# Layer 0's closing product in three passes, block-wise stores, and a first modulation summed in the two halves of the array

## The chip, the core and the metric

The kernel runs on one core of a Trainium2 chip. The metric is the device time of one launch in microseconds (us); the runs shown are the median of three. Engine names in the rows: PE is TensorE's matmuls and PEld its weight loads, DVE is VectorE, ACT is ScalarE, POOL is GpSimd, SP is the queue on which most transfers are issued.

## What is computed

Two blocks of a small transformer stand behind each other, in float32, with 256 latent tokens, 256 context tokens and a model width of 1024. Only three places of it matter here.

```
mod_l = split(silu(c) @ ada_w[l] + ada_b[l], 6)          # and mod_c from c_ctx
hl = modulate(x_lat, norm_g[l, 0], mod_l[0], mod_l[1])    # rms_norm(x) * (1 + scale) + shift
...
mix_c, mix_l = even_mixer(hc, hl, ...)                    # 4 mLSTM heads and 8 window-attention heads
x_lat = x_lat + mod_l[2] * (mix_l @ w_out[l])             # the closing product of the mixer
x_lat = x_lat + mod_l[5] * conv_ffn(modulate(x_lat, norm_g[l, 1], mod_l[3], mod_l[4]), ...)
```

Parts 0 and 1 of the first `mod` (shift and scale of layer 0, for latent and context) are needed before any product on `h` can start. In layer 0 the closing product `mix @ w_out[0]` is made for latent and context tokens, 512 columns; in layer 1 for the 256 latent ones. The second block ends in a layer norm and a gated sum, which gives the output.

## The kernel before

Everything lies feature-major: `x`, `h` and `mix` hold 8 blocks (index `k`, `KD` = 8) of 128 features by 512 tokens. A weight tile is 128 by 1024 (512 KB), that is 8 stationary blocks of 128 by 128 for one output block. Each engine has its own program, written out in order by hand; they meet in semaphores (`mark` raises one, `at` names the value to wait for).

**The weight ring.** All weight tiles come through `RING`, 7 places of 512 KB, in the order of the list `TILES`. `sync_program` issues tile t on SP when tile t-7 has been released; what releases it is named with the tile (its product, or the pass over it that takes its rest).

**Two ways to multiply.** `pe_product` (L246) multiplies in plain float32: each matmul is recorded as two LDWEIGHTS and two MATMUL. `pe_product3` (L264 to L266) makes three passes instead, on operands that are split beforehand in a rounded part (type fp32r) and the rest: rounded weights by rounded data, rounded weights by the rest of the data, rest of the weights by rounded data. Each of the three is one record. The split of a weight tile is an ACT copy (`act_round`, L273), then a subtraction on DVE (`dve_rest`, L279) or POOL (`pool_rest`, L285), into one of three pairs `HI`, `LO`.

**The start.** `pe_start` sums the first modulation: 16 tiles of `ada_first`, numbered from 0, per tile 8 matmuls with a stationary of 2 columns (the two conditions, `cs`) and 128 columns of the tile moving, into 2 rows of a bank (L393). Ahead of tile 12 stands the mean of the squares of x (L436). ACT copies the rows out after tiles 3, 7, 11 and 15 (L365); ahead of the last copy stand a table load and the two steps of the reciprocal root (L442, L444), by which DVE and POOL normalise x (L468, L464). At last PE turns the rows into columns with 16 small transposes (L398), DVE adds the bias (L417), forms the gains (L428) and scales `h` (L477), and the first product on `h` starts (L246).

**The end of the mixer.** The last head ends with the numerators (PE L853), the denominators (ACT L895) and divisions on DVE, the turned probabilities (PE L721, copies L747 and L749, scaled by DVE L676), the attention sums of 64 rows each (PE L731, two heads in turns in the two halves of the columns), `mixed_attention` (L976) and `mixed_heads` (L979). Then `pe_wout(0)` makes 8 output blocks of 8 plain matmuls each, block 0 at L1008 with its waits inside, blocks 1 to 7 by `pe_product`. After each block DVE adds it to x (L1054, `residual`), ACT squares (L1025), DVE sums the squares (L1038). In between DVE works through two pairs of modulation tiles, `dve_ada` (L335, L338). After the last block come a mean, a reciprocal root, and the modulated h, split in two, for the up product of the feed-forward (L1131 to L1133 for its first three tiles in one loop, then `pe_product3`).

**The end.** `pool_close` writes the last sum block by block (`closed`), and SP stores the whole output in one transfer when all 8 are closed.

## Time and profile before

| | before |
|---|---|
| median of the three runs, us (lowest, highest) | 1690.59 (1689.98, 1692.39) |
| the profiled execution's own time, us | 1693.57 |
| its span in the trace, us | 1692.3 |
| PE busy | 1593.9 us (94%) |
| DVE busy | 1098.3 us (65%) |
| ACT busy | 712.1 us (42%) |
| POOL busy | 463.6 us (27%) |

Where PE is busy for 94% of the span, the time gets shorter where PE's work gets less, or where PE waits and the wait goes. Busy shares don't tell which; the chain of waits and the timeline at the three places do. The times in the rows below count from the start of the span.

### The profile page before, as it was taken

Reading aid. Unit: us, or ns where it says so; the run is one execution under the profiler, and the core shown is the slowest. Engines: PE = TensorE matmul, PEld = TensorE weight load, DVE = VectorE, ACT = ScalarE, POOL = GpSimd, SP = SyncE. Lnnn points to the kernel's source line nnn. Section 1 sums busy time; section 2 is a strip of 40 time slices with the busy share of each in tenths; the row PEclk is TensorE's granted clock in tenths of the full one; section 3 lists DMA queues with packets and bytes.
Section 4 is the critical chain, followed back from the end, with each engine's and each line's share of the span. In section 5 each row is a group of like instructions: output and inputs, shape, how many; then the busy total and the mean of one; then the engine's idle time right before and its main releaser. Section 6 shows DMA issues by size and latency. Waiting matters only on the chain.

```text
span 1692.3 us, 24887 instructions
## 1 busy us (share of the span) xinstructions
PE 1593.9 (94%) x9516; PEld 1300.4 (77%) x9516; DVE 1098.3 (65%) x2015; ACT 712.1 (42%) x1333; POOL 463.6 (27%) x375
## 2 busy tenths in 40 slices
PE   7999999989999999988999999999999999999888
PEld 5555566448888888866667899998888888898777
DVE  4567887558877788747777788655454545453763
ACT  1432433143333332344442555544444444454544
POOL 1012102002222210115530111025555555522651
PEclk9899999999999999999999999999999999999999
DMA  9323213224333356502234455544333334344230
GB/s 346 138 99 113 99 64 137 100 74 147 138 137 140 148 203 209 196 33 100 88 113 162 172 186 178 187 176 132 133 135 129 134 127 135 120 136 148 94 131 26
DMA packets 63831, 231.23 MB, mean 137 GB/s; under 512 B 7408, under 2 KB 8432, under 8 KB 63456
## 3 DMA queue, kind: packets, MB, share of 16 engines
q1 hardware_dynamic: 60800, 218.65, 36.8%
q0 software_dynamic: 2192, 6.29, 1.1%
q10 hardware_dynamic: 720, 4.68, 0.7%
q8 instruction: 76, 1.25, 0.3%
q14 instruction: 43, 0.35, 0.1%
HBM read 228.55 MB, written 1.05 MB: 136 GB/s over the span
## 4 chain that ended last, share of the span: by engine, by line
PE 82%; DVE 8%; ACT 5%; issue 3%; POOL 1%; DMA 0%; ACTq 0%; DVEq 0%; POOLq 0%
PE ps L264 12%; PE ps L246 12%; PE ps L266 12%; PE ps L265 12%; PE ps L1241 4%; PE ps L1240 4%; PE ps L1239 4%; PE ps L254 2%; PE ps L731 2%; PE ps L393 2%; PE ps L721 2%; DVE big L676 2%; ACT big L657 2%; PE ps L624 1%; PE ps L308 1%
## 5 line engine op out<-in xcount | busy, mean ns | idle before, releaser
L279 DVE TENSOR_TENSOR weights_rest<-ring,weights_rounded 128x1024 fp32r<-128x1024 f32 x193 | 267.6, 1389 | 66.5 <-ACT weights_rounded L273 66.4
L273 ACT ACTIVATE weights_rounded<-ring 128x1024 fp32r<-128x1024 f32 x231 | 241.9, 1053 | 120.6 <-PE ps L1241 94.1
L266 PE MATMUL ps<-h_hi,weights_rest 128*128 128x512 f32 (+1 forms) x640 | 215.1, 336 | 0.0
L265 PE MATMUL ps<-h_lo,weights_rounded 128*128 128x512 f32 (+1 forms) x640 | 215.1, 336 | 0.0
L264 PE MATMUL ps<-h_hi,weights_rounded 128*128 128x512 f32 (+1 forms) x640 | 215.1, 336 | 0.0
L1225 POOL TENSOR_TENSOR big<-scratch 128x512 f32<-128x512 f32 (+1 forms) x44 | 64.2, 1460 | 406.4 <-DVE scratch L1211 406.4
L1165 ACT ACTIVATE scratch<-ps,vectors 128x512 f32<-128x512 f32 (+1 forms) x88 | 59.2, 672 | 191.4 <-PE ps L266 182.5
L285 POOL TENSOR_TENSOR weights_rest<-ring,weights_rounded 128x1024 fp32r<-128x1024 f32 x38 | 91.2, 2402 | 168.6 <-ACT weights_rounded L273 168.6
L246 PE MATMUL ps<-h,ring 128*128 128x512 f32 x288 | 131.4, 612 | 2.2 <-DVE h L477 2.2
L265 PEld LDWEIGHTS ps<-h_lo,weights_rounded 128*128 128x128 f32 x640 | 121.5, 190 | 12.6
L266 PEld LDWEIGHTS ps<-h_hi,weights_rest 128*128 128x128 f32 x640 | 121.5, 190 | 12.5
L264 PEld LDWEIGHTS ps<-h_hi,weights_rounded 128*128 128x128 f32 x640 | 121.5, 190 | 12.4
L338 DVE SCALAR_TENSOR_TENSOR ring<-ring,cond_rows 128x1024 f32<-128x1024 f32 x80 | 123.1, 1539 | 2.8
L1239 PE MATMUL ps<-hid_rounded,weights_rounded 128*128 128x512 f32 (+1 forms) x352 | 120.7, 343 | 3.8 <-DVE hid_rest L1300 3.8
L1241 PE MATMUL ps<-hid_rounded,weights_rest 128*128 128x512 f32 (+1 forms) x352 | 119.1, 338 | 0.0
L1240 PE MATMUL ps<-hid_rest,weights_rounded 128*128 128x512 f32 (+1 forms) x352 | 119.0, 338 | 0.0
L246 PEld LDWEIGHTS ps<-h,ring 128*128 128x128 f32 x288 | 55.9, 197 | 72.3 <-issue 69.6
L335 DVE SCALAR_TENSOR_TENSOR junk<-ring,cond_rows 128x1024 f32<-128x1024 f32 x80 | 102.3, 1278 | 1.0 <-POOL scratch L1066 1.0
L1208 DVE SCALAR_TENSOR_TENSOR scratch<-ps,vectors,scratch 128x510 f32<-128x510 f32 (+1 forms) x88 | 53.8, 611 | 63.7 <-ACT scratch L1165 63.6
L264 PE MATMUL ps<-x_hi,weights_rounded 128*128 128x256 f32 x280 | 83.4, 298 | 1.1 <-ACT scratch L1739 1.1
L264 PE MATMUL ps<-x_hi,a_rounded 128*128 128x256 f32 x248 | 74.6, 301 | 5.2 <-ACT scratch L1746 5.2
L266 PE MATMUL ps<-x_hi,weights_rest 128*128 128x256 f32 x280 | 79.1, 282 | 0.0
(366 smaller groups left out, 3916.3 us busy)
## 6 DMA issues: line engine op xcount, KB each, us to landing
ring<-in_up SPq DMA_DIRECT2D x88, 512.0 KB, 3.9
ring<-in_ada_rest SPq DMA_DIRECT2D x80, 512.0 KB, 4.5
ring<-in_a_in SPq DMA_DIRECT2D x80, 512.0 KB, 3.5
ring<-in_down SPq DMA_DIRECT2D x44, 512.0 KB, 3.7
ring<-in_even SPq DMA_DIRECT2D x20, 512.0 KB, 3.8
ring<-in_ada_first SPq DMA_DIRECT2D x16, 512.0 KB, 8.1
ring<-in_wout SPq DMA_DIRECT2D x16, 512.0 KB, 3.5
ring<-in_odd SPq DMA_DIRECT2D x16, 512.0 KB, 3.5
```

Of the source, the lines that this page charges most:

```text
L246: ins = te.matmul(bank[:, 0:n], w[:, k, :], rhs(k), start=k == 0, stop=k == KD - 1)
L264: te.matmul(bank[:, 0:n], wh[:, k, :], hi(k), start=k == 0, stop=False)
L265: te.matmul(bank[:, 0:n], wh[:, k, :], lo(k), start=False, stop=False)
L266: ins = te.matmul(bank[:, 0:n], wl[:, k, :], hi(k), start=False, stop=k == KD - 1)
L273: sc.activation(pair[0], place(*key), ACT.Copy).then_inc(*mark("rounded", *key))
L279: ve.tensor_tensor(pair[1], place(*key), pair[0].bitcast(F32), ALU.subtract).then_inc(*mark("rest", *key))
L285: po.tensor_tensor(pair[1], place(*key), pair[0].bitcast(F32), ALU.subtract).then_inc(*mark("rest_pool", *key))
L335: ve.scalar_tensor_tensor(JUNK, w, 1.0, CREP[:, 0:D], ALU.mult, ALU.mult, accum_out=SUMS[:, 2 * j:2 * j + 1]).then_inc(*mark("mod_products ...
L338: ve.scalar_tensor_tensor(w, w, 1.0, CREP[:, D:2 * D], ALU.mult, ALU.mult, accum_out=SUMS[:, 2 * j + 1:2 * j + 2]).then_inc(*mark("mod_sum ...
L1239: te.matmul(b, wh[:, e, :], hi, start=j == 0, stop=False)
L1240: te.matmul(b, wh[:, e, :], lo, start=False, stop=False)
L1241: ins = te.matmul(b, wl[:, e, :], hi, start=False, stop=j == FB - 1)
```

## The change

1. **Start.** `cs` becomes 64 columns for each `k` (2 with the conditions, 62 of zeros, cleared by POOL). The matmuls of even `k` write rows 0 to 63 of the bank and those of odd `k` rows 64 to 127, each half with its own columns of the array, and the halves are added later: the 16 turning steps become matmuls with 128 rows as stationary and a matrix `V_SUM` of two columns (ones in rows 0 and 64, and in rows 1 and 65) moving. They wait for the four copies one by one.
2. **Closing product of layer 0.** It is made in three passes. `mix` is split into `MIX_HI` (in the place of `h`, which is free by then) and `MIX_LO` (in place): ACT rounds the 8 blocks, POOL takes the rests of 0, 1, 2, 4, 5, 6 and DVE those of 7 and 3. The weight tiles are split too: rounded on ACT, the rests of tiles 0 to 2 on POOL, of 3 to 7 on DVE, three pairs in turn. Blocks 0 and 1 are made in one loop over `k`.
3. **Pairs for the up product.** Its first four tiles get pairs of their own in `BIG`, in both layers, since `HI` and `LO` are in use until the closing product ends.
4. **Stores.** SP stores each of the 8 output blocks when it is closed, and waits for the last.

```diff
@@ wout_tiles
-            tile(("wout", layer, b), f"wout{layer}", b, "product", "wout", layer, b)
+            tile(("wout", layer, b), f"wout{layer}", b, wout_rest(b) if layer == 0 else "product", "wout", layer, b)
@@ sync_program
             sp.wait_ge(*at("closed", 1, k))
-        sp.dma_start(out, xv[:, :, LAT]).then_inc(*mark("stored", step=16))
-        sp.wait_ge(*at("stored"))
+            sp.dma_start(out[:, k, :], xk(k)).then_inc(*mark("stored", k, step=16))
+        sp.wait_ge(*at("stored", KD - 1))
@@ pe_start
             for k in range(KD):
-                ins = te.matmul(BANK[b][0:2, 128 * (s % 4):128 * (s % 4) + 128], cs[:, 2 * k:2 * k + 2], w[:, k, :],
-                                start=k == 0, stop=k == KD - 1)
+                half = slice(64 * (k % 2), 64 * (k % 2) + 64)
+                ins = te.matmul(BANK[b][half, 128 * (s % 4):128 * (s % 4) + 128], cs[:, k, :], w[:, k, :],
+                                start=k < 2, stop=k >= KD - 2)
             ins.then_inc(*mark("product", "ada_first", s))
-        te.wait_ge(*at("rows_copied", 3))
-        for j in range(16):
-            ins = te.transpose(BANK[2][:, 2 * j:2 * j + 2], rows2[0:2, 128 * j:128 * j + 128], ident[0:2, 0:2])
+        for g in range(4):
+            te.wait_ge(*at("rows_copied", g))
+            for j in range(4 * g, 4 * g + 4):
+                ins = te.matmul(BANK[2][:, 2 * j:2 * j + 2], rows2[:, 128 * j:128 * j + 128], v(V_SUM, 2), start=True,
+                                stop=True)
@@ act_even
+        if i == AH - 1:
+            for b in range(2):
+                act_round(("wout", 0, b), pair(b), wout_free(b))
         act_exps(us)
...
+            if i == AH - 1 and t == 3:
+                for k in range(3):
+                    act_mix(k, at("mixed_heads", k))
             sc.wait_ge(*at("numerators", i, t))
...
         head_norm()
+        if i == AH - 1:
+            act_mix(4, at("mixed_attention", 0))
         weigh_copies(sc, 1, E, groups0(i), TB0, PT0, only=(5,))
+        if i == AH - 1:
+            for k in (5, 6, 7):
+                act_mix(k, at("mixed_attention", k - 4))
+            act_round(("wout", 0, 2), pair(2), wout_free(2))
+            act_mix(3, at("mixed_heads", 3))
@@ pool_even
+        if i == AH - 1:
+            for b in range(2):
+                pool_rest(("wout", 0, b), pair(b), wout_free(b))
+            for k in (0, 1, 2, 4, 5, 6):
+                mix_rest(po, k)
@@ new
+    def pe_wout_split():
+        for b in range(2):
+            te.wait_ge(*at(wout_rest(b), "wout", 0, b))
+        for x, k in enumerate((0, 1, 2, 4, 5, 6, 7, 3)):
+            te.wait_ge(*at("rest_pool" if mix_on_pool(k) else "h_rest", "mix", k))
+            hi, lo = mix_parts(k)
+            for b in range(2):
+                wh, wl = (v3(w, 128)[:, k, :] for w in pair(b))
+                te.matmul(BANK[b], wh, hi, start=x == 0, stop=False)
+                te.matmul(BANK[b], wh, lo, start=False, stop=False)
+                ins = te.matmul(BANK[b], wl, hi, start=False, stop=x == KD - 1)
+                if x == KD - 1:
+                    ins.then_inc(*mark("product", "wout", 0, b))
+        for b in range(2, KD):
+            if b >= 4:
+                te.wait_ge(*at("residual", 0, b - 4))
+            pe_product3(("wout", 0, b), pair(b % PAIRS), BANK[b % 4], TOK, lambda k: mix_parts(k)[0],
+                        lambda k: mix_parts(k)[1], wout_rest(b))
@@ act_wout
+            if layer == 0 and b + 3 < KD:
+                act_round(("wout", layer, b + 3), pair(b % PAIRS), wout_free(b + 3))
@@ dve_wout
+        if layer == 0:
+            mix_rest(ve, 7)
+            mix_rest(ve, 3)
         ve.wait_ge(*at("wout_cleared", layer))
...
+            if layer == 0 and b + 3 < KD:
+                dve_rest(("wout", layer, b + 3), pair(b % PAIRS), wout_free(b + 3))
@@ pool_wout
         po.memset(acc_o[:, 0:n], 0.0).then_inc(*mark("wout_cleared", layer))
+        if layer == 0:
+            pool_rest(("wout", 0, 2), pair(2), wout_free(2))
```

How the order moves on the engines for which PE waits. ACT at the end of the last head, before: the copies of the denominators (L895), the turned copies (L747), the heads' squares and norm (L903 to L915).

```order
L895 ACTIVATE scratch<-ps 128x2 x4
L747 ACTIVATE scratch<-ps 128x512
L903 ACTIVATE scratch<-scratch 128x128 x4
L747 ACTIVATE scratch<-ps 128x512
L909 ACTIVATE scratch<-scratch,eps 128x4
L911 ACTIVATE scratch<-scratch 128x4
L915 ACTIVATE scratch<-scratch 128x128 x4
L747 ACTIVATE scratch<-ps 128x512
```

The same place on ACT after the change (L895 is now L912, L747 is L758; L1037 rounds a block of `mix`):

```order
L912 ACTIVATE scratch<-ps 128x2 x3
L1037 ACTIVATE mix_hi<-mix 128x512 x3
L912 ACTIVATE scratch<-ps 128x2
L758 ACTIVATE scratch<-ps 128x512
L920 ACTIVATE scratch<-scratch 128x128 x4
L758 ACTIVATE scratch<-ps 128x512
L926 ACTIVATE scratch<-scratch,eps 128x4
L928 ACTIVATE scratch<-scratch 128x4
L932 ACTIVATE scratch<-scratch 128x128 x4
L1037 ACTIVATE mix_hi<-mix 128x512
L758 ACTIVATE scratch<-ps 128x512
L1037 ACTIVATE mix_hi<-mix 128x512 x3
```

Three roundings now stand ahead of the last of the four denominator copies, and one ahead of the last turned copy. DVE in the closing product, before (L335 and L338 are modulation tiles, L1054 the residual, L1038 the sum of squares), from the residuals of blocks 0 and 1 to that of block 2:

```order
L1054 SCALAR_TENSOR_TENSOR x<-ps,mod,x 128x256 x4
L1038 TENSOR_TENSOR scratch<-scratch 128x512
L335 SCALAR_TENSOR_TENSOR junk,mod_sums<-ring,cond_rows 128x1024
L338 SCALAR_TENSOR_TENSOR ring,mod_sums<-ring,cond_rows 128x1024
L335 SCALAR_TENSOR_TENSOR junk,mod_sums<-ring,cond_rows 128x1024
L338 SCALAR_TENSOR_TENSOR ring,mod_sums<-ring,cond_rows 128x1024
L1054 SCALAR_TENSOR_TENSOR x<-ps,mod,x 128x256 x2
L1038 TENSOR_TENSOR scratch<-scratch 128x512
```

The same place on DVE after (L1123 is the residual, L1104 the sum of squares, L282 the rest of a weight tile, L338 and L341 modulation tiles):

```order
L1123 SCALAR_TENSOR_TENSOR x<-ps,mod,x 128x256 x2
L282 TENSOR_TENSOR weights_rest<-ring,weights_rounded 128x1024
L1123 SCALAR_TENSOR_TENSOR x<-ps,mod,x 128x256 x2
L1104 TENSOR_TENSOR scratch<-scratch 128x512
L282 TENSOR_TENSOR weights_rest<-ring,weights_rounded 128x1024
L338 SCALAR_TENSOR_TENSOR junk,mod_sums<-ring,cond_rows 128x1024
L341 SCALAR_TENSOR_TENSOR ring,mod_sums<-ring,cond_rows 128x1024
L338 SCALAR_TENSOR_TENSOR junk,mod_sums<-ring,cond_rows 128x1024
L341 SCALAR_TENSOR_TENSOR ring,mod_sums<-ring,cond_rows 128x1024
L1123 SCALAR_TENSOR_TENSOR x<-ps,mod,x 128x256 x2
L1104 TENSOR_TENSOR scratch<-scratch 128x512
L282 TENSOR_TENSOR weights_rest<-ring,weights_rounded 128x1024
```

The rest of tile b+3 stands behind the residual of block b, and that of tile 5 behind two modulation tiles as well.

## Rows read from the trace of the kernel before

**Rows 1.** The page, part 4: the chain that ended last, by engine

```profile
PE 82%; DVE 8%; ACT 5%; issue 3%; POOL 1%; DMA 0%; ACTq 0%; DVEq 0%; POOLq 0%
```

**Rows 2.** Chain of waits in the first 110 us: start us, us, what

```profile
7.10 23.74 PE ps L393 x192
...
31.89 7.09 PE ps L393 x64
...
40.83 0.20 DVE mod L417
...
42.98 15.51 PE ps L246 x32
```

**Rows 3.** Timeline, 0 to 20 us: PE's weight load waits for a tile

```profile
14.95 5.11 PEld L393 LDWEIGHTS ps<-ring,scratch 128*2 128x2 f32 x48 [0.28 <-DMA ring<-in_ada_first]
```

**Rows 4.** Windows: PE, PEld, DVE, ACT, POOL busy (count), clock, DMA share, GB/s

```profile
14.00:20.00 6.00, 6.00 (x56) 4.46 (x55) 5.73 (x9) 0.59 (x1) 0.00 (x0) 1.00 1.03 412
...
43.00:46.00 3.00, 3.00 (x4) 1.45 (x5) 2.05 (x6) 2.43 (x5) 0.29 (x1) 0.50 0.98 368
```

**Rows 5.** Timeline, 20 to 40 us: the copy after tile 11, the normalising of x

```profile
30.87 0.59 ACT L365 ACTIVATE scratch<-ps 2x512 f32<-2x512 f32 x1 [6.40 <-PE ps L393]
...
34.15 5.83 DVE L468 TENSOR_TENSOR h<-x,rsqrt 128x512 f32<-128x512 f32 x6 [8.76 <-ACT rsqrt L444]
34.20 3.43 POOL L464 TENSOR_TENSOR h<-x,rsqrt 128x512 f32<-128x512 f32 x2 [33.33 <-ACT rsqrt L444]
```

**Rows 6.** Timeline from 38.5 us: the last three of L468

```profile
38.10 1.88 DVE L468 TENSOR_TENSOR h<-x,rsqrt 128x512 f32<-128x512 f32 x3
```

**Rows 7.** Timeline, 1166 to 1176 us, PE: sums in the halves of the columns

```profile
1170.43 1.31 PE L731 MATMUL ps<-big,scratch 128*64 128x256 f32 x16
```

**Rows 8.** Window on L398 alone: PE, PEld busy (count), clock, DMA share, GB/s

```profile
39.64:40.62 0.98, 0.97 (x16) 0.97 (x16) 1.00 0.84 313
```

**Rows 9.** Chain of waits, 285 to 400 us

```profile
304.26 6.87 PE ps L1008 x16
311.13 48.08 PE ps L246 x112
...
367.41 0.43 PE ps L1132
...
384.97 0.23 PE ps L264
...
390.41 0.23 PE ps L264
```

**Rows 10.** Timeline of ACT, 290 to 305 us: the last denominator copy

```profile
295.28 0.17 ACT L895 ACTIVATE scratch<-ps 128x2 f32<-128x2 f32 x1 [1.39 <-PE ps L853]
```

**Rows 11.** Timeline of DVE, 295 to 304 us: the last probabilities

```profile
298.75 1.12 DVE L676 TENSOR_SCALAR big<-big,stats 128x256 f32<-128x256 f32 x4
```

**Rows 12.** Groups of DVE by line and shape, 304 to 362 us: busy, mean ns

```profile
L1054 DVE SCALAR_TENSOR_TENSOR x<-ps,mod,x 128x256 f32<-128x256 f32 x16 | 7.0, 480 | 30.3 <-PE ps L246 30.0 <-PE ps L1008 0.3
L338 DVE SCALAR_TENSOR_TENSOR ring<-ring,cond_rows 128x1024 f32<-128x1024 f32 x4 | 4.9, 1224 | 0.1
...
L1038 DVE TENSOR_TENSOR scratch<-scratch 128x512 f32<-128x512 f32 x7 | 4.8, 681 | 0.0
L279 DVE TENSOR_TENSOR weights_rest<-ring,weights_rounded 128x1024 fp32r<-128x1024 f32 x3 | 3.5, 1217 | 0.0
```

**Rows 13.** Groups of ACT by line and shape, 304 to 362 us

```profile
L1025 ACT ACTIVATE scratch<-x 128x512 f32<-128x512 f32 x8 | 5.0, 630 | 51.6 <-DVE x L1054 51.6
L273 ACT ACTIVATE weights_rounded<-ring 128x1024 fp32r<-128x1024 f32 x3 | 2.9, 1041 | 0.0
```

**Rows 14.** The page, part 5: a weight tile's rest on POOL

```profile
L285 POOL TENSOR_TENSOR weights_rest<-ring,weights_rounded 128x1024 fp32r<-128x1024 f32 x38 | 91.2, 2402 | 168.6 <-ACT weights_rounded L273 168.6
```

**Rows 15.** DMA issues of the whole run: size, median us from issue to landing

```profile
big<-in_rpb POOLq DMA_DIRECT2D x32, 64.0 KB, 2.2
...
out<-x SPq DMA_DIRECT2D x1, 1024.0 KB, 5.4
...
scratch<-in_masks POOLq DMA_DIRECT2D x1, 256.0 KB, 3.1
```

More of the change, by code:

```diff
@@ L144, in build, with wout_rest @@
     ODD_ADA = [(68, 69), (70, 71), (72,), (73,)]
+    def wout_rest(b):
+        return "rest_pool" if b < 3 else "rest"
     def wout_tiles(layer):
@@ L359, in act_start @@
         sc.wait_ge(*at("vectors_in"))
-        sc.activation(cs, v(V_C, 16), ACT.Silu).then_inc(*mark("cond_act"))
+        sc.wait_ge(*at("cond_cleared"))
+        sc.activation(cs[:, :, 0:2], v3(v(V_C, 16), 2), ACT.Silu).then_inc(*mark("cond_act"))
         for g in range(4):
@@ L991, in pool_even, with wout_free, mix_parts @@
         pool_rope(("even", i), at("normed", "even", i, 0), q0[:, CTX:TOK], ROPE1, t2)
+        if i == AH - 1:
[3 more added lines that the diff above has]
+                mix_rest(po, k)
     FIRST = 3
     acc_o, sq_o = SCR[:, 0:TOK], [SCR[:, TOK:2 * TOK], SCR[:, 2 * TOK:3 * TOK]]
+    def wout_free(b):
+        return [at("product", "wout", 0, b - PAIRS)] if b >= PAIRS else []
+    def mix_parts(k):
+        return MIX_HI[:, k * TOK:(k + 1) * TOK], MIX_LO[:, k * TOK:(k + 1) * TOK]
@@ new lines, in act_mix, with mix_on_pool, mix_rest @@
+    def act_mix(k, event):
+        sc.wait_ge(*event)
+        sc.activation(mix_parts(k)[0], MIX[:, k * TOK:(k + 1) * TOK], ACT.Copy).then_inc(*mark("h_rounded", "mix", k))
+    def mix_on_pool(k):
+        return k % 4 < 3
+    def mix_rest(eng, k):
+        hi, lo = mix_parts(k)
+        eng.wait_ge(*at("h_rounded", "mix", k))
+        ins = eng.tensor_tensor(lo, MIX[:, k * TOK:(k + 1) * TOK], hi.bitcast(F32), ALU.subtract)
+        ins.then_inc(*mark("rest_pool" if mix_on_pool(k) else "h_rest", "mix", k))
@@ L998, in pe_wout @@
     def pe_wout(layer):
         n = TOK if layer == 0 else SEQ
-        order, waits = ((0, 1, 2, 4, 5, 6, 7, 3), {0: at("mixed_heads", AH - 2), 7: at("mixed_attention", AH - 1), 3: at(
-            "mixed_heads", AH - 1)}) if layer == 0 else ((0, 1, 2, 3, 4, 5, 6, 7), {0: at("mixed_global", 3),
-                                                         4: at("mixed_near", 2), 7: at("mixed_near", 3)})
-        w = v3(place("wout", layer, 0), 128)
-        te.wait_ge(*loaded("wout", layer, 0))
-        for x, k in enumerate(order):
-            if k in waits:
-                te.wait_ge(*waits[k])
-            ins = te.matmul(BANK[0][:, 0:n], w[:, k, :], mixk(n)(k), start=x == 0, stop=x == KD - 1)
@@ L1009, in pe_wout @@
-        ins.then_inc(*mark("product", "wout", layer, 0))
-        for b in range(1, KD):
-            if b >= 4:
-                te.wait_ge(*at("residual", layer, b - 4))
-            pe_product(("wout", layer, b), BANK[b % 4], n, mixk(n))
+        if layer == 0:
+            pe_wout_split()
+        else:
+            waits = {0: at("mixed_global", 3), 4: at("mixed_near", 2), 7: at("mixed_near", 3)}
+            for b in range(KD):
+                if b >= 4:
+                    te.wait_ge(*at("residual", layer, b - 4))
+                pe_product(("wout", layer, b), BANK[b % 4], n, mixk(n),
+                           lambda k, b=b: [waits[k]] if b == 0 and k in waits else [])
@@ L1089, in halves @@
                 yield k, s, c, slice(k * n + c, k * n + c + 256)
-    UP_THIRD = (rounded("up_rounded_3", "big", 9216, D), rounded("up_rest_3", "big", 10240, D))
+    MIX_HI, MIX_LO = rounded("mix_hi", "h", 0, KD * TOK), rounded("mix_lo", "mix", 0, KD * TOK)
+    UP_FIRST = [(rounded(f"up_rounded_{j}", "big", c, D), rounded(f"up_rest_{j}", "big", c + D, D))
+                for j, c in enumerate((5120, 7168, 9216, 1024))]
     def up_pair(j):
-        return UP_THIRD if j == FIRST else pair((j if j < FIRST else j - 1) % PAIRS)
+        return UP_FIRST[j] if j <= FIRST else pair((j - 1) % PAIRS)
     def up_free(layer, j):
-        if j == FIRST:
-            return [at("mixed_near", 3)] if layer else [at("mixed_heads", AH - 1)]
+        if j > FIRST + PAIRS:
+            return [at("product", "up", layer, j - PAIRS)]
         if j > FIRST:
-            return [at("product", "up", layer, j - (PAIRS if j > FIRST + PAIRS else PAIRS + 1))]
-        return [at("product", "down", 0, FB - 1)] if layer else []
+            return [at("product", "wout", layer, KD - 1)]
+        return [at("mixed_near", 3)] if layer else [at("mixed_heads", AH - 1)]
     def down_pair(j):
```

11 lines of the change are left out of this document (8 added, 3 removed).

## The prediction

> **What bounds the kernel now.** First I read the chain of waits by engine [rows 1]: PE carries 82% of it, so a change counts where it takes work from PE or ends a wait of PE. Then the same chain in order of time, at the three places.
>
> *Start.* PE sums 12 tiles in 23.74 us and the last 4 in 7.09, that is 1.77 each [rows 2]. The timeline shows PE waiting for a tile at 14.95 [rows 3]: from there to 30.84 there are nine tiles of 1.77, so this is tile 3. The transfers meanwhile run at 412 GB/s with their engines full [rows 4]: 0.524 MB lands each 1.27 us. PE is the slower of the two, and transfers are right behind it. After tile 11 come ACT's copy (30.87), the root, and DVE's normalising from 34.15 for 5.83 us [rows 5], to 39.98. The bias waits for the turned rows until 40.83, and PE starts its first product at 42.98 [rows 2], at the lower clock (0.50 of full in 43 to 46 us, [rows 4]).
>
> *Closing product.* 16 records of L1008 and 112 of L246 take 54.95 us [rows 9], 6.87 a block, without a wait. DVE and ACT wait for PE there (30.3 and 51.6 us of idle time, [rows 12, 13]).
>
> *End.* One store of 1 MB lands 5.4 us after its issue [rows 15], and nothing lies beside it.
>
> **Start, term by term.** Two sums in the two halves of the columns: L731 is the same form (64 columns each, in turns). Its 16 records [rows 7], twelve with 128 columns moving and four with 256, would take 12 x 0.11 + 4 x 0.22 = 2.2 us one after the other (0.11 is 7.09 / 64, [rows 2]); they take 1.31, less some 0.16 for the last one's tail: 1.9 times as fast. A tile then costs PE 0.93 us, below the 1.27 at which it lands. So PE follows the transfers: tile 11 lands at 14.95 + 8 x 1.27 = 25.1 and is summed at 26.2 instead of 30.84. The chain behind it is unchanged: 3.3 us from copy to normalising, 5.83 of normalising [rows 5], end at 35.4. The other branch: tile 15 lands at 30.2, is summed at 31.3; the turning is now 32 records (two per plain matmul) where there were 16 at 0.061 each [rows 8], 2.0 us; at 0.11 each it would be 3.5. The last eight wait for a copy of 0.6. It ends by 33.3, at the dear price by 34.8, before 35.4 both times: the doubled turning costs nothing, because DVE's normalising hides it; without that cover it would cost up to 2. The bias starts at 35.4 instead of 40.83: **5.4 us**. What is late next is the clock. PE now stands nearly idle from 33.3 to 37.6 (before: 40.8 to 43.0), and in the 15.51 us of the first 32 records [rows 2] at 0.43 each (6.87 / 16, [rows 9]) there are already 1.75 us of lower clock. It can last as long again or vanish: -1.75 to +1.75, I take **-0.5**. The wider copies (128 rows for 2) move the same 512 columns and cost nothing; POOL's clearing lies before the vectors land.
>
> **Closing product.** Three passes: from the first record of up tile 3 to that of tile 4 it is 390.41 - 384.97 = 5.44 us for 24 matmuls [rows 9], a block of the same size. Eight blocks: 43.6 against 54.95, a gain of 11.4. Against it stand the waits:
> - *Before the product.* ACT was free from 293.89 to 295.28 [rows 10]. Three roundings of 0.6 (a 512-column copy, [rows 13]) now end at 295.7 and delay the last denominators, on which DVE's chain to the last copy hangs: 0.5. The roundings and rests of weight tiles 0 and 1 fall where ACT waits for an output and for DVE, and are hidden: without that cover 2.1.
> - *POOL beside DVE.* While POOL normalised its two blocks, three of DVE's took (5.83 - 1.88) / 3 = 1.32 us each; with POOL idle, 1.88 / 3 = 0.63 [rows 5, 6]. POOL now takes three rests of about 1.2 (half of 2402 ns, [rows 14]) from 294.5 to 298.2 or later, and L676 stands at 298.75 with 1.12 us [rows 11]. If it falls beside POOL wholly it doubles: 0 to 1.2, I take 0.7. The Trainium skill ("SBUF — State Buffer", section "SBUF: two separate sides") says that DVE and GpSimd take a shared port pair in turns, as an exclusive lock for a whole instruction. By that rule each of the four L676 could wait out a whole POOL rest, and the sum would be worse by up to 4 us; the rows show a doubling, and POOL should be through by then.
> - *Inside.* With P the end of blocks 0 and 1 (10.9 us after the start): residual 0.9, square 0.63, rounding 1.04, rest 1.22 [rows 12, 13] make tile 3 ready at P + 3.9, needed at P + 5.4. Residual 1, square, rounding and rest 4: P + 7.75, needed at P + 10.9. Then four modulation passes of 1.22 and residual 2, its square, the rounding of 5 and its rest: P + 16.5, needed at P + 16.35. That is the tightest place: 0.2. Tiles 6 and 7 are ready at about P + 20.5 and P + 24.5, needed at P + 21.8 and P + 27.2. `mix` 7 and 3 are needed 8.2 us after the start, DVE has them at about 5.
> - *After it.* The rests for the up product reach into the last residual: 0.3.
>
> Sum: 11.4 - 0.5 - 0.7 - 0.2 - 0.3 = **9.7 us**. The ring is no bound: tile 3 is issued when the first modulation tile of this stage is summed, some 6 us before its rounding. Ends: nothing lost, 11.4; or start late by 3 and DVE's work late for three blocks by 1 each: 5. The separate pairs move no wait of PE, since the up product's first tiles were rounded at the same place before: 0.
>
> **Stores.** The last one is 128 KB. The nearest rows are 64 KB with 2.2 and 256 KB with 3.1 [rows 15]; I take 2.6 for 5.4: **2.8 us**, ends 2.3 and 3.2. The other seven lie beside the closing blocks. The Trainium skill ("DMA: Bandwidth & Descriptors") gives a fixed cost of about 2.0 us and 436 GB/s; that makes 2.3, an estimate, and the sum 0.3 better.
>
> **Sum.** 5.4 - 0.5 + 9.7 + 2.8 = 17.4. The profiled execution (1693.57, its span and 1.3 around it) becomes 1676.2; it lies 3.0 above the median of the runs, 1690.59, which becomes **1673.2**.
>
> **Rivals.**
> - *A, the first sums gain little.* If PE waits for tiles at the lower clock, a tile costs it 1.86, tile 11 is summed at 29.4 and the turned rows come last: gain 0 to 2 there, time 1677 to 1678.5. For it: PE now has gaps between tiles. Against: when it slows, it falls behind the transfers and has no gaps left.
> - *B, the preparation doesn't keep up.* If DVE's passes beside POOL take 1.5 times as long, tiles 5, 6 and 7 are late by 1 to 2 us each, and the product's start by 3: gain 5, time 1677 to 1681. For it: a margin below zero at tile 5. Against: DVE is idle for 30 us of this stage.
> - *C, more than the sum.* Clock and POOL cost nothing or give back: 1669 to 1670.5.
> - *D, slower.* The lower clock stays through the closing product. At the lower level a pass takes 0.43, not 0.227 [rows 9]: 192 x 0.2 = 39 us more, net 22 slower, 1712. It decides once the lower level covers 85 of the 192 passes (17.4 / 0.2). Against it: PE goes into the product from work at full clock, and never waits long in it.
> - *E, no change:* only if start and product both fail.
>
> **How the numbers follow.** Forecast (1670.5 to 1677) 0.60, A 0.12, B 0.18, C 0.06, D 0.03, E 0.01. The predicted time is the forecast's. 1669 to 1680 leaves out D, E and the far end of B, with a tail on either side, about 0.1 to 0.15. A measurement tells 0.2% (3.4 us) from no change: faster 0.95, same 0.02, slower 0.03.
>
> **What would show it.** Right: L365's third copy near 26.3, L417 near 35.5; the records of the first sums in pairs, with waits for `ring` between tiles; PE's closing product near 44 us with at most a short wait before block 5; the last landing about 2.6 us after its issue. Wrong: L417 released by PE's turned rows (A), waits of PE for `weights_rest` before blocks 5 to 7 or a long stretch of DVE behind POOL near 299 us (B), a clock of 0.5 inside the product (D).

## The result, and the profile after

The changed kernel takes 1672.34 us in the median of four runs (1670.31 to 1673.68), the kernel before 1690.64 beside it. The ratio is 0.9894, with a 95% interval from 0.988 to 0.9908: 18.3 us faster, predicted were 17.4. The same kernel once more, `a0_after` below, gave 0.9896 [0.9881, 0.991].

The profiled execution is the slowest of the four (1673.68, span 1672.3). By its page PE still carries the chain that ended last, with 81% against 82% [rows 1]. The three places follow, each read against its rows of before.

**Start.** The chain of waits, first 57 us (start, us, what), against [rows 2]:

```profile
2.12 12.70 DMA ring<-in_ada_first
14.86 4.18 PE ps L402 x48
19.06 8.57 DMA ring<-in_ada_first
...
28.80 3.81 PE ps L402 x64
32.61 5.03 PE ps L408 x32
37.66 0.20 DVE mod L428
...
39.81 16.50 PE ps L249 x32
```

The transfers now stand where PE's sums stood: two stretches of DMA, 21.3 us together. The timeline of PE shows the sums (L402) waiting for tiles. The last column is the idle time before a group and what ended it:

```profile
14.86 6.21 PE L402 MATMUL ps<-ring,scratch 128*64 128x128 f32 x80 [0.81 <-DMA ring<-in_ada_first]
21.26 1.09 PE L402 MATMUL ps<-ring,scratch 128*64 128x128 f32 x16 [0.18 <-DMA ring<-in_ada_first]
23.83 1.09 PE L402 MATMUL ps<-ring,scratch 128*64 128x128 f32 x16 [1.48 <-DMA ring<-in_ada_first]
...
26.40 1.09 PE L402 MATMUL ps<-ring,scratch 128*64 128x128 f32 x16 [0.19 <-DMA ring<-in_ada_first]
```

Tiles 3 to 8 come at the pace of the transfers: (21.26 - 14.86) / 5 = 1.28 us. Tile 9 comes 2.57 after tile 8, one slot late, and tiles 10 and 11 keep that distance. So the sum of tile 11 begins at 26.40, and its copy stands at 27.54 where the prediction had 26.3. The copy and what hangs on it, answering to [rows 5] (first row ACT, the others DVE):

```profile
27.54 0.60 ACT L372 ACTIVATE scratch<-ps 128x512 f32<-128x512 f32 x1 [5.82 <-PE ps L402]
```

```profile
30.83 5.85 DVE L479 TENSOR_TENSOR h<-x,rsqrt 128x512 f32<-128x512 f32 x6 [5.54 <-ACT rsqrt L455]
37.66 0.19 DVE L428 TENSOR_TENSOR mod<-ps,vectors 128x32 f32<-128x32 f32 x1 [0.98 <-PE ps L408]
```

In this execution the bias (L428) stood 0.98 us idle behind the turned rows, at 37.66 instead of 40.83 [rows 2]. That is 3.2 us sooner; predicted were 5.4.

**Clock.** Windows of the same kernel (PE, PEld, DVE, ACT, POOL busy with counts, granted clock, DMA share, GB/s), against the second line of [rows 4]:

```profile
34.60:39.80 5.20, 3.02 (x16) 2.96 (x16) 4.08 (x10) 1.57 (x4) 1.56 (x3) 0.51 1.03 417
39.80:44.90 5.10, 5.09 (x6) 2.17 (x7) 2.08 (x6) 2.46 (x6) 0.32 (x1) 0.50 0.86 353
```

From 34.6 to 44.9 us PE ran at 1.2 GHz, three times as long as before at this place, so the first 32 records took 16.50 us instead of 15.51. They end at 56.31, against 42.98 + 15.51 = 58.49 before: 2.2 us are left of the start in this execution.

**Closing product.** PE's groups by line from 299.5 to 343.1 us (busy, mean ns, idle before), where [rows 9] had 54.95 us:

```profile
L267 PE MATMUL ps<-mix_hi,weights_rounded 128*128 128x512 f32 x48 | 18.7, 389 | 0.0
```

The groups of the other two passes, L268 and L269, have the same figures. The loop over the first two blocks (L1056 to L1058) has 48 records with 6.2 to 6.3 us for each of its lines. There is no idle time ahead of any pass. The chain has the product's start and the last residual:

```profile
299.52 0.24 PE ps L1056
...
343.52 0.47 DVE x L1123
```

From start to last residual it takes 343.52 - 299.52 = 44.0 us. Before it was 359.64 - 304.26 = 55.38; the start is in [rows 9], and the last residual in the same chain is

```profile
359.64 0.48 DVE x L1054
```

**End.** The DMA issues of the last 30 us, and the chain's last row, against [rows 15]:

```profile
out<-x SPq DMA_DIRECT2D x8, 128.0 KB, 1.9
```

```profile
1669.66 0.72 POOL x L2118
```

The span ends at 1672.3, 1.9 us behind the last block. The last block of before, in its chain:

```profile
1686.06 0.72 POOL x L2043
```

There it was 1692.3 - (1686.06 + 0.72) = 5.5. That gives 3.6; predicted were 2.8.

### The profile page after: what moved, and what is told of

It is laid out like the page before. It is cut to its first block, busy times and chain, and to the rows that moved or that the text cites. A ratio compares the mean times of both kernels' runs of the same rounds, so it can differ in the third digit from the quotient of the medians.

```text
span 1672.3 us, 25099 instructions
## 1 busy us (share of the span) xinstructions
PE 1572.5 (94%) x9596; PEld 1310.1 (78%) x9596; DVE 1109.3 (66%) x2022; ACT 724.2 (43%) x1349; POOL 476.7 (29%) x385
## 3 DMA queue, kind: packets, MB, share of 16 engines
HBM read 228.55 MB, written 1.05 MB: 137 GB/s over the span
## 4 chain that ended last, share of the span: by engine, by line
PE 81%; DVE 8%; ACT 5%; issue 3%; DMA 1%; POOL 1%; SPq 0%; ACTq 0%; DVEq 0%; POOLq 0%
PE ps L267 13%; PE ps L269 12%; PE ps L268 12%; PE ps L249 9%; PE ps L1314 4%; PE ps L1315 4%; PE ps L1316 4%; PE ps L257 2%; DVE big L687 2%; PE ps L742 2%; PE ps L732 2%; ACT big L668 2%; PE ps L311 1%; PE ps L635 1%; DMA ring<-in_ada_first 1%
## 5 line engine op out<-in xcount | busy, mean ns | idle before, releaser
L282 DVE TENSOR_TENSOR weights_rest<-ring,weights_rounded 128x1024 fp32r<-128x1024 f32 x192 | 267.9, 1397 | 72.7 <-ACT weights_rounded L276 72.7
L268 PE MATMUL ps<-h_lo,weights_rounded 128*128 128x512 f32 (+1 forms) x640 | 215.0, 336 | 0.0
L269 PE MATMUL ps<-h_hi,weights_rest 128*128 128x512 f32 (+1 forms) x640 | 215.0, 336 | 0.0
L288 POOL TENSOR_TENSOR weights_rest<-ring,weights_rounded 128x1024 fp32r<-128x1024 f32 x41 | 98.4, 2402 | 177.2 <-ACT weights_rounded L276 177.2
L268 PEld LDWEIGHTS ps<-h_lo,weights_rounded 128*128 128x128 f32 x640 | 121.5, 190 | 12.6
L269 PEld LDWEIGHTS ps<-h_hi,weights_rest 128*128 128x128 f32 x640 | 121.5, 190 | 12.5
L341 DVE SCALAR_TENSOR_TENSOR ring<-ring,cond_rows 128x1024 f32<-128x1024 f32 x80 | 123.1, 1539 | 2.8
L338 DVE SCALAR_TENSOR_TENSOR junk<-ring,cond_rows 128x1024 f32<-128x1024 f32 x80 | 102.1, 1276 | 0.4 <-POOL scratch L1137 0.4
L268 PE MATMUL ps<-x_lo,weights_rounded 128*128 128x256 f32 x280 | 79.7, 285 | 0.0
L269 PE MATMUL ps<-x_hi,weights_rest 128*128 128x256 f32 x280 | 79.7, 284 | 0.0
```

Source lines behind the costliest of these rows:

```text
L268: te.matmul(bank[:, 0:n], wh[:, k, :], lo(k), start=False, stop=False)
L269: ins = te.matmul(bank[:, 0:n], wl[:, k, :], hi(k), start=False, stop=k == KD - 1)
L282: ve.tensor_tensor(pair[1], place(*key), pair[0].bitcast(F32), ALU.subtract).then_inc(*mark("rest", *key))
L288: po.tensor_tensor(pair[1], place(*key), pair[0].bitcast(F32), ALU.subtract).then_inc(*mark("rest_pool", *key))
L338: ve.scalar_tensor_tensor(JUNK, w, 1.0, CREP[:, 0:D], ALU.mult, ALU.mult, accum_out=SUMS[:, 2 * j:2 * j + 1]).then_inc(*mark("mod_products ...
L341: ve.scalar_tensor_tensor(w, w, 1.0, CREP[:, D:2 * D], ALU.mult, ALU.mult, accum_out=SUMS[:, 2 * j + 1:2 * j + 2]).then_inc(*mark("mod_sum ...
```

## The experiments

### The three parts one by one

Each part alone on top of the kernel before, all three on one chip.

`e1_stores` stores by block and changes nothing else:

```diff
-        sp.dma_start(out, xv[:, :, LAT]).then_inc(*mark("stored", step=16))
-        sp.wait_ge(*at("stored"))
+            sp.dma_start(out[:, k, :], xk(k)).then_inc(*mark("stored", k, step=16))
+        sp.wait_ge(*at("stored", KD - 1))
```

> The kernel before with the block-wise stores alone. In the profile after the change the last store of 128 KB landed 1.9 us after its issue, and before the change the one store took 5.4. Theory (the end is an independent term): 3.5 us faster, last landing 1.9 us after issue, everything ahead unchanged. Rival (seven earlier stores cost something beside the closing blocks, or the issue of the last one queues behind them): less than 2.5 us faster, and closing blocks more than 3.74 us apart.

Measured: 1685.86 against 1690.03, ratio 0.9975 [0.9964, 0.9985], 4.2 us faster (2.5 to 6.1 by the interval), where 3.5 were expected. The trace has it at the place: the last block is closed at 1681.82 + 0.72, the span ends at 1684.5, 2.0 behind it instead of 5.5. The last closing blocks start 3.74 us apart, so the earlier stores hold nothing up and the rival is out.

`e2_wout` has the product in three passes and the separate pairs, with the old start and the old store:

```diff
-            tile(("wout", layer, b), f"wout{layer}", b, "product", "wout", layer, b)
+            tile(("wout", layer, b), f"wout{layer}", b, wout_rest(b) if layer == 0 else "product", "wout", layer, b)
...
+    def pe_wout_split():
```

> The kernel before with the closing product in three passes and the separate pairs, and with the start and the store as before. Theory (passes times 0.227 us, ACT's roundings delay the start of the product by 0.5 to 0.9): the product from its first record to the last residual takes 44.0 us instead of 55.4, the product starts 0.5 to 0.9 later than in the kernel before apart from differences of the clock, and the whole is 10.5 us faster (9.5 to 11.5), a stretch of lower clock more or less adding or taking 1.7. Rival (part of the 11.4 us belongs to the earlier start): below 9 us.

Measured: 1676.38, ratio 0.992 [0.9906, 0.9933], 13.6 us faster (11.3 to 15.9 by the interval), above the 9.5 to 11.5 that were expected; the rival, below 9, is out. This execution and that of `e1_stores` reach the last head within 0.01 us of each other (L853 at 288.06, here L858 at 288.05), which makes them a clean pair. The chain of `e1_stores`:

```profile
288.06 4.48 PE ps L853 x40
...
301.56 6.87 PE ps L1008 x16
...
356.94 0.48 DVE x L1054
```

The chain of `e2_wout`:

```profile
288.05 2.92 PE ps L858 x26
...
301.91 0.23 PE ps L1050
...
345.90 0.47 DVE x L1117
```

The product begins 301.91 - 301.56 = 0.35 us later and takes 43.99 instead of 55.38.

Little of the 0.35 is ACT's. Its three roundings end just as the last denominators are ready: DVE starts on them at 292.81 instead of 292.77, 0.04 later. The rest comes from two DVE instructions that stand beside POOL's rests of `mix`. The first (L977) takes 0.24 us instead of 0.16. The second is the first L675, 0.38 instead of 0.15, and it ends when POOL does:

```profile
295.14 0.38 DVE L675 TENSOR_TENSOR stats<-stats 128x1 f32<-128x1 f32 x1
```

```profile
291.75 3.75 POOL L1039 TENSOR_TENSOR mix_lo<-mix,mix_hi 128x512 fp32r<-128x512 f32 x3 [7.21 <-ACT mix_hi L1031]
```

Net gain at the last residual: 11.04 us, where the prediction's term was 9.7. The measured 13.6 lies above it, with 11.04 just outside its interval. The two traces differ by 12.45 when the last block is closed (1682.54 against 1670.09); the 1.4 in between come after this place. `e1_stores` has 3.4 us more of the lower clock in that part (34.1 against 30.7), which can be worth up to 1.7; no run isolates it.

`e3_start` has the new start alone:

```diff
-                ins = te.matmul(BANK[b][0:2, 128 * (s % 4):128 * (s % 4) + 128], cs[:, 2 * k:2 * k + 2], w[:, k, :],
-                                start=k == 0, stop=k == KD - 1)
+                half = slice(64 * (k % 2), 64 * (k % 2) + 64)
+                ins = te.matmul(BANK[b][half, 128 * (s % 4):128 * (s % 4) + 128], cs[:, k, :], w[:, k, :],
+                                start=k < 2, stop=k >= KD - 2)
```

> The kernel before with the start alone. Theory (transfers and the turning bound it: tile 11 is summed near 27.5, the turned rows come last): the bias starts near 37.7 instead of 40.83, and the first product's 32 records end about 2.2 us earlier (56.3). Time 2 to 3 us faster, plus or minus 3.4 by how long the lower clock lasts further on. Rival (the shorter low stretches near 75 and 90 us in the profile after the change were caused by the earlier start): 5 us faster and more, with low stretches near 75 and 90 us of 3.4 us each in this profile as well.

Measured: 1686.43, ratio 0.9979 [0.997, 0.9988], 3.6 us faster (2.0 to 5.1 by the interval), where 2 to 3 were expected, with the bias near 37.7. The bias in its timeline of DVE:

```profile
36.73 0.18 DVE L423 TENSOR_TENSOR mod<-ps,vectors 128x32 f32<-128x32 f32 x1
```

Here the bias has no bracket: it follows the normalising (30.95, for 5.85 us) at once, 0.9 us sooner than in the first profile of the changed kernel. The first product's 32 records end at 38.59 + 16.28 = 54.87, in `e1_stores` at 43.07 + 15.67 = 58.74: 3.9 us sooner. So the first profile of the changed kernel, with 2.2, showed less than this part is usually worth.

The three gains add up to 4.2 + 13.6 + 3.6 = 21.4 us, 3 more than all three bring together. Most of the surplus goes with the clock. Over the runs of this study the time of one and the same kernel falls by some 1.06 us for each 0.001 of mean granted clock, and the runs of `e1_stores` (0.9869 in the mean) and `e2_wout` (0.9865) had more of it than those of the kernel before beside them (0.9856), those of `e3_start` less (0.9844). Brought to one clock by this figure, the gains are 2.6, 12.2 and 4.9, together 19.7, and that of `a0_after` is 18.9. These are estimates from the times and clocks of all runs; single runs lie 0.5 us around them. Within that the parts add up: `e2_wout` lies 1.1 above its trace instead of 2.6, and `e1_stores` 0.9 below its own.

### The changed kernel once more, and three ways to mend its start

`a0_after` is the changed kernel again, on the chip of the next three kernels.

> The changed kernel once more, on the chip and in the call of the next three, so that they can be compared with it. Theory: 18 us below the kernel before. The bias of the first modulation starts at 36.6 us, when DVE's normalising ends, if TensorE's clock falls behind the turning, and at 37.7 if it falls inside it, as in the first profile of this kernel (0.213 us a record instead of 0.112).

Measured: 1671.01 (1670.38 to 1672.63) against 1688.59. The clock fell at 35.8, when the turning was nearly through, and the bias stood behind the normalising. Its chain at the start and at the last residual:

```profile
36.72 0.11 DVE mod L428
...
38.74 15.96 PE ps L249 x32
...
341.88 0.47 DVE x L1123
```

Its 32 records end at 54.70. In four of the six profiled executions with this start (`e3_start`, `a0_after`, `e7_mix_late`, `e8_pad_tile5`) the normalising sets the bias; in the first profile and in `e10_fill_only` the turned rows come last, by 0.98 and 0.26 us. So this one is of the more frequent kind, and the sum below is read from it.

`e4_turn_early` turns groups 0 to 2 of the rows among the sums:

```diff
+            if s in (6, 10, 15):
+                turn({6: 0, 10: 1, 15: 2}[s])
...
+        turn(3).then_inc(*mark("rows_turned"))
```

> The turning of groups 0 to 2 of the rows stands ahead of tiles 6, 10 and 15, so that only 8 of 32 records are left behind the last copy. Theory (turned rows came last in the first profile, DVE's normalising 1 us before them): the bias starts at 36.6 to 36.7 wherever the clock falls, 1.0 us sooner than in the first profile of the changed kernel and not sooner than where the clock fell later; the whole 0 to 1 us shorter. Rival (turning is not what sets the bias): nothing. Rival 2 (24 records of 0.11, that is 2.7 us, now delay tiles 6, 10 and 15 past their landing): copy 2 and so the normalising come up to 1 us later, since a tile takes PE 0.9 of the 1.27 us at which it lands.

Measured: 1671.38 (1668.42 to 1673.46), ratio 0.9893 [0.9875, 0.9912], no difference that can be told. The bias stands at 36.78. What the early turning would save where the clock falls inside it, as in the first profile, this execution does not show. Tile 11's copy came at 27.65 against 27.57, so the early turning was hidden behind the waits for tiles, and rival 2 is out.

`e5_root_early` also computes the mean and the root ahead of the copy behind tile 11:

```diff
-            if g == 3:
+            if g == 2:
...
+            if s == 11:
+                te.wait_ge(*at("consts_in", "first"))
+                pe_mean((0, 0), ACC, TOK, at("square_sum", "x", KD - 1))
```

> As the one before, and the mean is computed ahead of tile 11, while its load is awaited, with ACT's root ahead of the copy behind that tile. Theory: with the turning out of the way DVE's normalising sets the bias; it hangs on mean, root (1.28 + 0.70 + 0.64 us) and the copy of 0.6 ahead of them, so it starts 1.3 to 2 us sooner, and the bias at 34.6 to 35.4: the whole 1.3 to 3 us below the changed kernel. Rival (something else, as the first weights of the product or the last tiles' sums, comes last): below 0.5 us. The last tile is summed at 32.6, its copy ends at 33.3, 8 records follow: 34.3, so that this bound lies just below.

Measured: the bias stands at 35.35, 1.4 us sooner, as expected. The whole took 1670.61 (1669.22 to 1672.94), ratio 0.9893 [0.9878, 0.9908]: not the 1.3 to 3 us less that were expected, but no difference that can be told. The chain says where it went:

```profile
35.35 0.20 DVE mod L432
...
37.51 16.80 PE ps L249 x32
```

and the windows of the same execution:

```profile
19.30:36.40 17.10, 15.25 (x206) 13.19 (x202) 12.40 (x19) 4.76 (x7) 3.90 (x3) 1.00 1.03 408
36.40:43.20 6.80, 5.69 (x7) 2.52 (x8) 3.18 (x8) 3.56 (x8) 1.42 (x3) 0.50 1.03 423
```

The product begins 1.2 us sooner (37.51 against 38.74 in `a0_after`), but more of it lies in the stretch at the lower clock, and its 32 records take 16.80 us instead of 15.96. They end at 54.31, only 0.4 sooner.

`e6_fill` adds three matmuls, whose result is not read, in PE's gap:

```diff
+        for _ in range(3):
+            te.matmul(BANK[3], mean_d, xv[:, 0, :], start=True, stop=True)
```

> As the one before, with three fp32 matmuls of 512 columns more behind the turning, into a bank that is not read, which fill some 2.7 us of PE's idle time before the first product. Theory (the lower clock in the first product follows PE's idle time from 33 to 38 us): less of the 10.2 us of lower clock that the first profile of the changed kernel shows, the first 32 records of the product in 14 to 15.5 us instead of 16.5, whole 1 to 2.5 us less than without. Rival (PE is still partly idle from 15 to 33 us, and that suffices): the same 16.3 to 16.7 us, the lower clock only begins at another time; difference to the one before below 0.5.

Measured: 1667.62 (1665.58 to 1669.20), ratio 0.9873 [0.9859, 0.9888]. All four runs lie below all four of `a0_after` and of `e5_root_early`; against the latter the median is 3.0 us lower, more than the 1 to 2.5 expected. Chain and windows of the profiled execution:

```profile
35.17 2.68 PE ps L416 x6
37.85 13.73 PE ps L249 x32
```

```profile
36.00:43.00 7.00, 7.00 (x18) 3.17 (x17) 3.44 (x8) 3.81 (x8) 1.68 (x3) 1.00 1.02 420
```

Until 35.2 us this kernel does what the one before it does. Then PE works instead of standing, the clock stays at 2.4 GHz through the product's start, and 32 records take 13.73. The first product ends at 51.58, 3.1 us sooner than in `a0_after`, though it starts only 0.9 sooner. It has the lowest median of the study. The profiled execution is the fastest of its four, at a mean granted clock of 0.990; the others have 0.986 to 0.988, so this good case is not the rule.

### How sure the filler is

`e9_fill_one` is the same with one filling matmul (`range(1)`).

> The kernel with early turning and root, and one filling matmul (0.9 us) instead of three (2.7 us). Theory (the fall of the clock at 36.4 us follows the idle stretch before the product): one matmul ends at 36.1, the bias of 35.35 lets the product start at 37.5 instead of 37.85. If one is enough, there is no lower clock between 19 and 70 us, the 32 records take 13.73 us, and the whole is 0 to 0.5 us below the run with three. Rival: 1.4 us of idle time is still too much, the clock falls and the records take 15.5 to 16.8 us, 2 to 3 us more. Then the whole stands near that without a filler.

Measured: 1670.63 (1665.51 to 1672.44), ratio 0.9875 [0.9856, 0.9893]. One of five runs took 1665.51, at a mean granted clock of 0.990 (that of the profiled `e6_fill`); the other four took 1670.4 to 1672.4 at 0.985. In the profiled execution, one of those four, the granted clock was 0.51 from 37.8 to 41.2 us and the records took 15.66. By time and clock four of the five runs are of the rival's kind, and one is of the good kind.

Whether three fillers do better than one is not shown. The ratios, each against the kernel before on its own chip, are 0.9873 with three and 0.9875 with one. The two profiled executions differ ahead of the filler as well: with one the granted clock was 0.50 from 13.9 to 20.7 us too, with three it was 1.00 from 7 us on.

`e10_fill_only` puts the three matmuls into the changed kernel, with nothing moved.

> The changed kernel with the three filling matmuls behind the turning, and nothing else: turning and root stand where the change has them. Theory: DVE's normalising sets the bias at 36.6 to 36.8, the product starts at 38.6; PE turns until 36.2 (full clock), fills to 38.9, so that the product starts at 38.9 and its 32 records take 13.75 to 14.5 us: the first product ends near 52.8 instead of 54.7 to 56.3, whole 2 us below the changed kernel. Rival: the idle gap of 32.6 is filled but the clock falls over the gaps of the first sums (4 us of waits for the ring before); then no gain.

Measured: 1670.84 (1669.15 to 1674.03), ratio 0.9881 [0.9862, 0.9899]: the 2 us less that were expected did not come. The profiled execution shows why the filler alone can miss. Chain and window:

```profile
32.40 4.28 PE ps L408 x32
36.68 5.33 PE ps L412 x6
42.01 13.83 PE ps L249 x32
```

```profile
35.20:42.00 6.80, 6.80 (x15) 3.70 (x15) 5.33 (x14) 4.04 (x8) 1.88 (x3) 0.50 1.02 417
```

The clock fell at 35.2, in the middle of the turning and ahead of the filler. The filler then ran at 1.2 GHz, took 5.33 us instead of 2.7, and held the product back from 38.7, where `a0_after` has it, to 42.01. So a gap before the product is one way to the lower clock and not the only one: here PE had been at work since 27.5 us, last with the turning. The rival named gaps of PE among the first sums; this execution does have them (0.80 to 1.28 us, until 23.78), but so have those where the clock fell later. What decides between the two cases at 35 us is open.

### Where the product's preparation has slack

`e7_mix_late` moves ACT's first three roundings of `mix` behind the heads' norm:

```diff
-            if i == AH - 1 and t == 3:
-                for k in range(3):
-                    act_mix(k, at("mixed_heads", k))
...
+            for k in range(3):
+                act_mix(k, at("mixed_heads", k))
```

> The changed kernel with ACT's roundings of mix 0 to 2 behind the heads' norm instead of ahead of the last denominators. Theory (those roundings delay DVE's chain by 0.5 and POOL's rests beside it slow L681 by 0.2): the product's first record comes 0.5 to 0.8 us sooner after the first record of the numerators (L864) than in the changed kernel, where it was 299.52 - 285.68 = 13.84, that is 13.0 to 13.3; the product itself then waits for the rests of mix, whose first is ready later, by 0 to 1.5 us. Rival (the roundings are hidden): 13.8 again.

Measured: 1672.67, one run. By the timeline of PE the product now starts 298.58 - 284.32 = 14.26 us after the last head's numerators begin, against 297.65 - 283.87 = 13.78 in `a0_after`: later, not sooner by 0.5 to 0.8. Half of the theory held. The probabilities behind the denominators (L687) stand 0.37 sooner in relation to that start, and the first L681, which took 0.38 us beside POOL in `a0_after`, takes 0.15 with POOL idle. But the timeline of ACT shows the roundings as one block ahead of the last copy of the attention, which starts at 296.44 instead of 294.48 in `a0_after`, and PE waits for that copy:

```profile
294.36 2.17 ACT L1036 ACTIVATE mix_hi<-mix 128x512 fp32r<-128x512 f32 x4
```

```profile
297.15 1.08 PE L742 MATMUL ps<-scratch,big 128*64 128x256 f32 x8 [1.77 <-ACT scratch L758]
```

`e8_pad_tile5` puts three passes of DVE ahead of the rest of weight tile 5; they only multiply two tiles that are there:

```diff
+            if layer == 0 and b == 2:
+                ve.wait_ge(*at("mod_products", 27))
+                for x in range(3):
...
+                    ve.tensor_tensor(JUNK, CREP[:, 0:D], CREP[:, D:2 * D], ALU.mult).then_inc(*mark("padded", x))
```

> The changed kernel with three passes of DVE more (1024 columns, product of two tiles that are there, result not read; 1.22 us each, 3.7 in all) ahead of the rest of weight tile 5. Theory: in the profile of the changed kernel that rest ended 1.05 us before block 5, where the prediction had it at -0.15 us. Then PE now waits 3.7 - 1.05 = 2.6 us before block 5, and again nothing before blocks 6 and 7 or up to 1 us, and the last residual comes 2.6 to 3.6 us later. Rival (the order of DVE's work lets other passes fall back and the rest is not what is late): no wait before block 5, but up to 3.7 before 6 or 7.

Measured, in the trace of one run: PE waits 1.6 us in the whole product, all of it for this rest, where 2.6 were expected:

```profile
L267 PE MATMUL ps<-mix_hi,weights_rounded 128*128 128x512 f32 x48 | 18.8, 391 | 1.6 <-DVE weights_rest L282 1.6
```

It ends at 326.54, 28.7 us after the product's start at 297.85, in `a0_after` at 324.07, 26.2 after 297.89: 2.5 us later for 3.73 of padding, since DVE used to wait there for ACT's rounding:

```profile
322.84 1.23 DVE L282 TENSOR_TENSOR weights_rest<-ring,weights_rounded 128x1024 fp32r<-128x1024 f32 x1 [1.05 <-ACT weights_rounded L276]
```

The last residual comes 1.85 us later (343.69 - 297.85 = 45.84 against 341.88 - 297.89 = 43.99). So of 2.5 the margin took 0.65; the prediction had it at -0.15, and the expectation of this run at 1.05. The place is the tight one, as forecast, and it costs nothing as it stands. Blocks 6 and 7 never waited.

## Why the prediction came out right

The time was right to 0.9 us, and the mechanism was right in the main, but not every size. The start gave 1.2 us less than its term, and five other terms together gave 2.3 us more than theirs. That these errors offset each other is luck. The product itself, the largest term, was right to 0.1 and owes nothing to it. The sums below take `e1_stores` for the old start and product, and `a0_after` for the new one.

| term | predicted | measured | where |
|---|---|---|---|
| bias of the first modulation | 5.4 | 4.2 | 40.91 to 36.72 |
| clock in the first product | -0.5 | -0.2 | 15.67 to 15.96 for 32 records, and 0.1 in the step between |
| ACT's roundings ahead of the last denominators | -0.5 | -0.04 | `e2_wout` |
| DVE beside POOL | -0.7 | -0.31 | `e2_wout`, L977 and L675 |
| the product itself | 11.4 | 11.4 | 55.38 to 43.99 |
| tile 5 and the last residual | -0.5 | 0 | no wait in PE's groups |
| last landing | 2.8 | 3.5 | 5.5 to 1.9 or 2.0 |

The rows of `e1_stores` that the first two take:

```profile
40.91 0.20 DVE mod L417
...
43.07 15.67 PE ps L246 x32
```

The terms add to 18.5; the measured medians give 17.6 and 18.3. Up to the last residual the two traces agree with it: 356.94 - 341.88 = 15.06, and 4.2 - 0.2 - 0.35 + 11.4 = 15.05.

*The start: the step "So PE follows the transfers", with tile 11 landing at 25.1, was mis-sized.* The pace of 1.28 is right, and so is that PE now waits for the transfers. But one tile more passes before tile 11: tile 9 comes a slot late in the first profile, and `a0_after` has its sums of tiles 9, 10 and 11 at the same places (23.87, 25.15, 26.43). Copy, root, normalising and bias follow from it as forecast, 1.3 us later each. Why tile 9 is late is open. That the doubled turning "costs nothing" is right in this execution and wrong in the first one: 32 records took 5.03 us there, because each costs 0.11 at 2.4 GHz and 0.21 at 1.2, not the 0.061 taken. The upper bound of 3.5 was for the higher clock alone. Rival A, that the turned rows come last, happened in that execution at 1 us and not at the 3 to 5 that its time needed. Its own price does not follow either: nine tiles of 1.86 from 14.95 end at 31.7 and not at 29.4, so the 29.4 holds only for a lower clock over part of that stretch.

*The clock* was rightly the term with two signs. What the prediction took as a cost of the edit differs from one execution to the next. In the records of before, 6.8 us more of lower clock lie near 77 and 90 us than in `e1_stores`, which runs the same code until its end:

```profile
76.80:83.60 6.80, 6.80 (x10) 2.86 (x9) 2.34 (x6) 1.75 (x10) 1.55 (x3) 0.50 0.30 120
```

```profile
77.50:80.90 3.40, 3.40 (x6) 1.85 (x6) 1.91 (x5) 1.35 (x9) 1.55 (x3) 0.50 0.45 181
```

Near 90 us it is 6.9 (from 90.4) against 3.5 (from 91.1).

The closing product stands at 304.26 in the one and at 301.56 in the other. So the profiled execution of before lay 2.7 us late at this place by its clock alone. The prediction was made against that execution and then set down by 3.0 to the median, which is why this did no harm.

*The closing product: what was taken off it was too dear.* The term of 0.7 was for L676 (now L687) beside POOL, and that did not happen: in the first profile POOL's three rests end at 293.1 and the four passes of L687 begin at 294.01, taking 1.12 as in [rows 11]. POOL holds up two smaller instructions ahead of it instead, by 0.31 in `e2_wout`, and ACT's roundings cost 0.04 against 0.5. The tight place at tile 5 has 0.65 of margin instead of -0.15. One reason is in the rows of `a0_after`: block 0 is finished ahead of block 1, so its residual starts at 308.16 and not at P, 297.89 + 10.9 = 308.8. Nothing reached into the last residual. Rival B, the preparation that doesn't keep up, is out: it would need waits of PE in the product, and there are none. Rival D is out by the same rows.

*The stores* landed in 1.9 us where the prediction took 2.6; the nearest row was a load of 64 KB with 2.2. The estimate from the page "DMA: Bandwidth & Descriptors" of the Trainium skill, 2.3, was nearer and still too long; the page fits its figures on transfers that GpSimd issues, and these are issued on SP.

## What to carry to other kernels

A phase that waits for transfers is dated by the landing of its last tile; count the tiles from a row close to that tile, since one slip of a slot moves everything behind it. Work that waits on the lower clock is worth looking at where PE stands before a product: an edit that starts the product 1.2 us sooner gave back 0.8 of it to the clock, and in a good execution three matmuls without a use brought back 2.7. Before a piece of work is moved off one chain, look at what it is then queued ahead of on its engine.

## What the runs showed of the hardware

- **The clock can fall while PE is at work.** In `e10_fill_only` it fell at 35.2 us amid matmuls that had run since 27.5 us (PE busy for 7.74 of the last 7.80). In `e1_stores` it fell at 77.4, during the last of eight matmuls with a moving operand of 4 rows (L505), when PE had been busy without a gap from 60 us on. And it did not fall in `e6_fill` at 36 us, where `e5_root_early`, with 2.7 us less of PE's work there, has it at 36.4. What decides is not shown. The time of a run follows it: in the runs of `e9_fill_one`, 0.990 of mean granted clock went with 1665.51 us and 0.985 with 1670.4 to 1672.4.
- **DVE waits out an instruction of POOL, but not every one does.** In the first profile of the changed kernel the same rest of `mix` on DVE takes 0.69 us alone and 2.48 beside POOL's rest of a weight tile:

```profile
300.70 0.69 DVE L1045 TENSOR_TENSOR mix_lo<-mix,mix_hi 128x512 fp32r<-128x512 f32 x1
302.17 2.48 DVE L1045 TENSOR_TENSOR mix_lo<-mix,mix_hi 128x512 fp32r<-128x512 f32 x1 [0.78 <-ACT mix_hi L1037]
```

```profile
301.69 2.40 POOL L288 TENSOR_TENSOR weights_rest<-ring,weights_rounded 128x1024 fp32r<-128x1024 f32 x1 [0.46 <-ACT weights_rounded L276]
```

  POOL ends at 304.09, DVE 0.56 later. POOL's 2.40 is its usual time for such a rest [rows 14], so DVE waited the instruction out, and the two did not share. The Trainium skill ("SBUF — State Buffer", section "SBUF: two separate sides") has an exclusive lock for a whole instruction, among others for DVE instructions with two inputs in SBUF beside a GpSimd instruction that reads SBUF; here the trace agrees. L675 in `e2_wout` is a second case, with two inputs and 0.38 us instead of 0.15. The prediction held a doubling against it, from the normalising; that can be read as the same waits spread over three instructions. Beside POOL's second three rests (296.31 to 300.06) a reciprocal on DVE, with one input, took 1.74 us, as it does in `e1_stores` with POOL idle. L676, for which the prediction feared a wait, has one input too, and at this place no profile has it beside POOL.
- **Matmuls in the two halves of the columns** work with plain float32 operands too: where tiles were at hand, the last four took 3.81 us (64 records of L402 in the chain above), 0.95 a tile against the 1.77 of [rows 2].
